# Half-width level products in a chunked delta-rule scan, with the next step's preparation in the state rounds

## The reference, cut to what matters

```python
def step(S, inp):
    r_t, w_t, k_t, v_t, a_t, b_t = inp
    Sa = jnp.einsum('bhij,bhj->bhi', S, a_t)
    S = S * w_t[:, :, None, :] + Sa[..., None] * b_t[:, :, None, :] + v_t[..., None] * k_t[:, :, None, :]
    y = jnp.einsum('bhij,bhj->bhi', S, r_t)
    return S, y
```

## Time and profile before

| what | value |
|---|---|
| median of 3 runs | 3108.72 us (3098.69 to 3109.58) |
| the profiled execution | 3100.7 us, span 3098.9 us |
| mean granted share of TensorE's 2.4 GHz | 0.947 |
| the scan's matmuls | first 741.3, last 1365.5 us |

### The profile page before, as it was taken

The page is one execution under the profiler, slowest core; times in us unless marked ns, Lnnn a source line. Parts: engine busy times, 40 slices in busy tenths (PEclk is TensorE's granted clock), DMA queues, the critical chain, the costliest instruction groups (busy, mean ns, idle before and its releaser), DMA issues. The chain is left out here.

```text
span 3098.9 us, 90983 instructions
## 1 busy us (share of the span) xinstructions
PE 2755.5 (89%) x39070; PEld 2134.9 (69%) x39070; DVE 2072.2 (67%) x3228; ACT 1459.6 (47%) x2171; POOL 324.5 (10%) x258
## 2 busy tenths in 40 slices
PE   5999987996999999974952999999999999999994
PEld 3455545665988998962532788888777777888872
DVE  3344076776656665635248888888888888888873
ACT  3211165664222232223131666666666666666663
POOL 0000000002112211204200000111101000101000
PEclk8999999998999999986975999999999999999997
DMA  4113051003221112032313999999999999999984
GB/s 127 35 41 141 20 214 43 0 0 83 68 62 44 44 50 79 4 136 85 128 69 119 333 310 315 310 316 315 307 315 303 310 301 324 317 312 306 324 273 152
DMA packets 282900, 544.78 MB, mean 176 GB/s; under 512 B 13296, under 2 KB 96880, under 8 KB 282576
## 3 DMA queue, kind: packets, MB, share of 16 engines
q1 hardware_dynamic: 273728, 505.62, 47.4%
q0 software_dynamic: 8848, 34.08, 4.2%
HBM read 487.23 MB, written 52.43 MB: 174 GB/s over the span
## 5 line engine op out<-in xcount | busy, mean ns | idle before, releaser
L1630 DVE SCALAR_TENSOR_TENSOR arena<-arena 128x1024 f16<-128x1024 f32 x768 | 904.2, 1220 | 101.5 <-ACT arena L1575 101.1
L1529 PE MATMUL ps<-arena 128*128 128x160 f16 x12288 | 855.4, 233 | 7.8 <-DVE arena L1639 3.3
L1529 PEld LDWEIGHTS ps<-arena 128*128 128x128 f16 x12288 | 851.9, 98 | 12.4 <-issue 9.6
L1575 ACT ACTIVATE arena<-arena 128x1024 f16<-128x1024 f32 x768 | 766.7, 1049 | 149.0 <-PE ps L1554 147.9
L876 PE MATMUL ps<-arena 64*64 64x64 f32 (+1 forms) x14080 | 505.5, 225 | 29.6 <-DVEq L1027 20.2
L876 PEld LDWEIGHTS ps<-arena 64*64 64x64 f32 x14080 | 487.4, 137 | 33.6 <-DVEq L1027 20.4
L1546 PE MATMUL ps<-arena 128*128 128x512 f16 x1536 | 366.6, 390 | 0.0
L389 PE MATMUL ps<-arena 128*128 128x512 f16 (+1 forms) x1584 | 285.7, 344 | 0.7 <-ACT arena L235 0.7
L1546 PEld LDWEIGHTS ps<-arena 128*128 128x128 f16 x1536 | 143.1, 100 | 185.1 <-issue 40.3
L389 PEld LDWEIGHTS ps<-arena 128*128 128x128 f16 x1584 | 154.9, 98 | 131.7 <-ACT arena L235 1.2
L1596 ACT ACTIVATE arena<-ps 128x160 f32<-128x160 f32 x256 | 77.7, 304 | 257.4 <-PE ps L1529 257.2
(11 more groups left out here) (216 smaller groups left out, 2952.9 us busy)
## 6 DMA issues: line engine op xcount, KB each, us to landing
arena<-w_gate SPq DMA_DIRECT2D x128, 1024.0 KB, 5.4
arena<-w_up SPq DMA_DIRECT2D x128, 1024.0 KB, 5.5
arena<-w_down SPq DMA_DIRECT2D x128, 1024.0 KB, 6.6
arena<-feat SPq DMA_DIRECT2D x120, 256.0 KB, 4.5
feat<-arena SPq DMA_DIRECT2D x20, 640.0 KB, 3.0
arena<-w_in SPq DMA_DIRECT2D x21, 512.0 KB, 4.0
arena<-tokens SPq DMA_DIRECT2D x20, 512.0 KB, 4.1
feat<-arena POOLq DMA_DIRECT2D x1, 7680.0 KB, 22.8
```

The lines of the kernel that those rows point to most:

```text
L1529: ins = pe.matmul(ps[:, o:o + SLOTS], part(4 * c + 2 * w + k // 4, pw) [:, k % 4, f * P:(f + 1) * P], xT2[:, px, k], start=(k == 0 and i = ...
L1575: act.activation(split[k % SPLIT][:, q * PW:(q + 1) * PW], ring[k % RING][:, q * PW:(q + 1) * PW], ACT.Copy, scale=W_SCALE).then_inc(w_hi, 1)
L1630: v.scalar_tensor_tensor(split[k % SPLIT][:, WCH + q * PW:WCH + (q + 1) * PW], ring[k % RING][:, q * PW:(q + 1) * PW], W_SCALE, split[k % ...
```

## The change

Level products stream only the columns that can be nonzero. `half_of(x, l, second)` picks, in every pair of blocks of width m, the first or the second block; `packed` gives PSUM the 32 columns side by side. The stationary operand keeps its 64 columns. `prod` becomes a buffer of its own for each level, cleared once at the start, so that ScalarE writes only the half that changes; `gu` takes its place in the state rounds. VectorE adds only the half. The width-1 level is computed from PSUM for both directions ahead of the masks, and each mask is one instruction of 1024 elements. `sums` is split: `rates` stand inside levels 2 to 4, `running` in state round 0, `blocks` in state round 1; the exponentials follow the copies of state round 0. `vb`, `bt` and `kt` have one buffer each, and the loads of `vb` come last. The tokens follow the `ax` of both directions.

```diff
-                                ins = heads(at_bank(d, 0, i), alv[d][:, l, i], inv[d][:, i])
+                                ins = heads(packed(at_bank(d, 0, i, C // 2), l), alv[d][:, l - 1, i],
+                                            half_of(inv[d][:, i], l, d == 1))
...
                             for i in range(NI):
+                                x = prod(d, l)[:, i]
                                 if l < NL:
-                                    heads(at_bank(d, 1, i), invT[d][:, i], prod[d][:, i])
-                                ins = heads(at_bank(d, 2, i), prod[d][:, i], invT[d][:, i])
+                                    heads(packed(at_bank(d, 1, i, C // 2), l), invT[d][:, i], half_of(x, l, d == 1))
+                                ins = heads(packed(at_bank(d, 2, i, C // 2), l), x, half_of(invT[d][:, i], l, d == 0))
...
-                            act.copy(flat(prod[d]), bank(4 * d)).then_inc(prod_ready[d], 1)
+                            act.copy(half_of(flat(prod(d, l)), l, d == 1),
+                                     packed(bank(4 * d, W // 2), l)).then_inc(prod_ready[d], 1)
...
                             if l < NL:
-                                v.tensor_tensor(flat(inv[d]), flat(inv[d]), bank(4 * d + 1), ALU.add)
-                            v.tensor_tensor(flat(invT[d]), flat(invT[d]), bank(4 * d + 2), ALU.add)
+                                x = half_of(flat(inv[d]), l, d == 1)
+                                v.tensor_tensor(x, x, packed(bank(4 * d + 1, W // 2), l), ALU.add)
+                            x = half_of(flat(invT[d]), l, d == 0)
+                            v.tensor_tensor(x, x, packed(bank(4 * d + 2, W // 2), l), ALU.add)
...
-                            pool.wait_ge(masks_ready[d], 3 * g + 1)
+                            pool.wait_ge(masks_ready[d], 3 * g + 2)
...
+                if g:
+                    v.wait_ge(tok_psum[d], NTOK * g)
+                v.tensor_tensor(flat(bt[d]), t1, ebk, ALU.mult)
```

More of the change, by code:

```diff
@@ L778, in build @@
         o2 += 2 * W
+        prod_a = at(o2, 2 * (NL - 1), NI, C)
+        o2 += 2 * (NL - 1) * W
         assert o2 <= E_ + 2 * KD * P + 2 * (NT + 3)
         o1 = R1
-        alv = [at(o1 + d * 6 * W, len(LEVELS), NI, C) for d in range(2)]
-        o1 += 12 * W
+        alv = [at(o1 + d * NL * W, NL, NI, C) for d in range(2)]
+        o1 += 2 * NL * W
         tokb = [at(o1 + d * W, NI, C) for d in range(2)]
@@ L788, in build @@
         o1 += 2 * W
-        prod = [at(o1 + d * W, NI, C) for d in range(2)]
+        prod_b = at(o1, 2, NI, C)
         o1 += 2 * W
+        gu = [at(o1 + d * RT * C, RT, C) for d in range(2)]
+        o1 += 2 * RT * C
         assert o1 <= B_
@@ L796, in build @@
         cin_free = [sem(f"cin_free{d}") for d in range(2)]
+        vb_in = [sem(f"vb_in{d}") for d in range(2)]
         zeroed = sem("zeroed")
@@ L836, in flat, with prod, half_of, packed @@
             return x.rearrange("p a b -> p (a b)")
+        def prod(d, l):
+            return prod_a[:, 2 * (l - 1) + d] if l < NL else prod_b[:, d]
+        def half_of(x, l, second):
+            m = LEVELS[l]
+            return x.rearrange("p (a w b) -> p a w b", w=2, b=m)[:, :, int(second)]
+        def packed(x, l):
+            return x.rearrange("p (a b) -> p a b", b=LEVELS[l])
         with nc.Block() as block:
@@ L941, in step @@
                             for f in range(RT):
-                                ins = heads(at_bank(d, 0, f), invT[d][:, 2 * f + place(d, c)], prod[d][:, f])
+                                ins = heads(at_bank(d, 0, f), invT[d][:, 2 * f + place(d, c)], gu[d][:, f])
                             ins.then_inc(u_psum[d], 1)
@@ L1055, in step @@
                             if l < NL:
-                                v.tensor_tensor(flat(inv[d]), flat(inv[d]), bank(4 * d + 1), ALU.add)
-                            v.tensor_tensor(flat(invT[d]), flat(invT[d]), bank(4 * d + 2), ALU.add)
+                                x = half_of(flat(inv[d]), l, d == 1)
+                                v.tensor_tensor(x, x, packed(bank(4 * d + 1, W // 2), l), ALU.add)
+                            x = half_of(flat(invT[d]), l, d == 0)
+                            v.tensor_tensor(x, x, packed(bank(4 * d + 2, W // 2), l), ALU.add)
                             v.drain().then_inc(inv_ready[d] if l < NL else invT_final[d], 1)
-                        if more and l in (1, 2):
-                            sums(g + 1, l - 1)
-                        if more and l in (3, 4):
-                            blocks(g + 1, l - 3)
+                            if more and 2 <= l <= 4:
+                                rates(g + 1, d, l - 2)
                     for c in range(2):
+                        if more:
+                            for d in range(2):
+                                if c == 0:
+                                    running(g + 1, d)
+                                else:
+                                    blocks(g + 1, d)
                         for d in range(2):
@@ L1087, in _ @@
                 for d in range(2):
-                    sums(0, d)
+                    running(0, d)
+                for part in range(3):
+                    for d in range(2):
+                        rates(0, d, part)
+                    v.drain()
                 for d in range(2):
```

140 lines of the change are left out of this document (77 added, 63 removed).

## The result

The changed kernel takes **3055.14 us** (median of 4 runs, 3053.32 to 3057.18); the kernel before, timed beside it, 3107.01 us (3098.69 to 3109.58). The ratio is 0.9838, with an interval of 0.9817 to 0.9858: faster by 1.6%. Its profiled execution took 3056.16 us. The medians differ by 51.9 us, the two profiled executions by 44.5: the one before was some 6 us quicker than its median. What the traces explain is the 44.5.

What follows compares the result with a forecast made beforehand. The prediction took TensorE's own work to set a scan step, with 3 to 6 us idle. Its terms, -27 + 8 - 7 - 8 + 1 = -33 us from the profiled 3100.7 us, gave 3068 us, range 3035 to 3100.

Steps and rivals of the forecast that it cites:

- Narrow products: Level products moving 32 columns: the 64-column weight load sets 58.3 ns a pair, so no gain in TensorE's own time.
- first rival: Level products at 32 moved columns are cheap, 29 ns a pair, giving 2980 us; chance 0.13.
- Front: Start of a scan step: TensorE's wait ahead of the second transposition goes, 2.7 us a step, -27 us.
- Transitions: Between levels: direction 1's update and POOL end slightly late without the tokens as cover, 0.8 us a step, +8 us.
- second rival: Broken runs on ScalarE and VectorE cost full width, level transitions take +28 us, about 3093 us; chance 0.11.
- State rounds: End of a step: `running` and `blocks` fit VectorE's idle time there, costing nothing; 5 us without the cover.
- Clock: Steps below full granted clock: the dips go with the front's 2.7 us wait, -7 us (0 to -8).
- Input loads: Loads moved to a step's end and the pair products: less "issue" idle time on TensorE, -8 us (0 to -17).
- hits half as many of these stalls: Beside the moved loads, TensorE issues a pair in 109 instead of 58 ns, so it meets half the "issue" stalls.
- Start: Before the scan: direction 0's `rates` no longer fill the wait for direction 1's loads, +1 us (0 to +2).
- third rival: 32-column products count like idle time, the clock falls, 64- and 128-column work behind slows; 3200 us at half; chance 0.07.
- better bounds: The whole kernel's time with every term at its favourable end, put at 3040 us.

Runs made afterwards that it cites:

- new_front_only: The kernel before with only the new front (width-1 level and invT of both directions ahead of the masks, POOL behind them): 3083.95 us, ratio 0.9921.
- wide_cover: The changed kernel with 64 moved columns and the tokens back between the two directions' ax, one of them at level 5: 3049.52 us, ratio 0.9813.
- after_again: The changed kernel timed once more, as a control, with nothing altered: 3054.53 us, ratio 0.9825.
- narrow_streams_only: The kernel before with level products moving only the first 32 columns, the rest left out, products added times zero: 3153.81 us, ratio 1.0129.
- old_front: The changed kernel with the front's old order (direction 0 masked first, POOL starting behind that mask), 32-column streams kept: 3135.05 us, ratio 1.0076.
- thin: The changed kernel moving 8 columns in every level product, the rest left out, products added times zero: 3243.42 us, ratio 1.0440.
- widths: The changed kernel moving 64, 32, 16, 8 and 32 columns in levels 1 to 5, the rest left out: 3142.91 us in one run.
- extra_loads: The changed kernel with ten more 256 KB transfers a step during the levels, into a spare tensor nobody reads: 3076.96 us, ratio 0.9898.

## Why the prediction was right, and where not

The time came out 13 us under the forecast, inside the range, for the reasons given; -33 us were forecast from the profiled execution, and 44.5 came. Term by term:

- **Narrow products, 0: right.** 58 ns at 8 to 64 moved columns, 33.5 with half the load, and no loss with 64 columns again. The first rival (2980 us) is out. The reading of the earlier trace rows was loose: 1.85 and 1.95 us contain the last pass's own duration, and by their starts the passes lie 112 ns apart in both rows, so an eighth of the columns saved nothing, and half of the price is 56 ns, not 58.
- **Front, -27: right.** The wait is gone in every step; put back, it costs 3.0 us a step. What the prediction looked for behind it was POOL's delivery, which was in time. It did not see that POOL's later start would stretch VectorE's preparation, had that stayed in the levels: 15 us in new_front_only. The change moves both, and its trace has no such wait.
- **Transitions, +8:** +5.6 measured against wide_cover (0.56 us a step), +6.8 by the sum below. The second rival is out: broken runs cost 422 and 377 ns.
- **State rounds, 0: right.** The wait there is 0.5 us a step as before, and VectorE's idle time took `running` and `blocks`.
- **Clock, -7: about right.** Three of eight steps were below 1.00, one of nine is now, where the prediction wanted none. The stretches at the low level sum to 20.8 us in the scan before and 6.4 after; at 7.5 us for 17.6 us of them, the 14.4 us fewer make 6.
- **Input loads, -8: mis-sized**, as the least certain term. "Issue" fell by 12.8 us. The step "hits half as many of these stalls" failed: next to none was left, 0.7 us here and 2.0 in the trace of after_again.
- **Start, +1:** +2.3.

The terms but the start forecast -34 for the scan, where -43.9 was measured. Counted from the starts of all 17,920 matmuls in each of the two scans, with a pass at 29 ns (54.5 with 128 moved columns) at the full clock, the scan's change is made up of -27.5 for the idle time of the front's listed waits, -12.8 for that under "issue", -3.9 for what the listed waits cost beyond their listed idle time, -6.5 for the low clock, and +6.8 for all that is in no list, where the transitions are. So the prediction left out the 3.9 us, 0.2 us a wait, and made the loads 5 us too small. Outside the scan, the 3.0 us behind it stand in no term. The better bounds that the prediction lists give -52, so 3049 us and not 3040; the measured time lies within either.

The **third rival** did not come about, but its mechanism is shown, and the prediction priced it on the wrong work. It took the narrow products as immune and charged only the 64- and 128-column work behind them; in fact the narrow products themselves nearly double, from 58 ns to 99 (narrow_streams_only), 101 (old_front) and 106 (thin). With 32 columns, whether it decides hangs on idle time ahead of the thin streams: the narrow streams alone, with the 2.7 us wait left in, made the kernel 1.3% slower. In the change, the new front is the cover that the narrow streams need: with the old one they cost 38 us. What the halved copies and additions of ScalarE and VectorE are worth, no run shows alone.

## What to carry to other kernels

Before narrowing what a matmul moves, set a row with few moved columns beside one with many at the same load: if the starts are as far apart, only a smaller load will help, and the thinner stream makes the clock easier to lose. When work of VectorE is reordered, look for what POOL will overlap with then, not only for whether POOL delivers in time. Parts of one change need not add up: narrow streams alone were a loss, the new front alone gave half of the gain, and a version with wide streams and the tokens left in their place was at least as fast as the whole.

## What the runs showed of the hardware

- The price of a pair of passes that its weight load sets (64 columns of float32) follows the granted clock: 58 ns a pair at 2.4 GHz, 106 at 1.2 GHz, with 8 moved columns; with 64 it is 58 (widths) and 108 (the tokens of old_front, 32 pairs from 971.04 to 974.49).
- The granted clock fell without idle time: with 8-column streams TensorE issued through the levels without a gap and still had 41 of 75 us at 1.2 GHz. With 32-column streams it fell after 2.8 us idle, in seven steps of ten, and stayed low through level 1 and the tokens behind it, where 64-column streams had it back within level 1.
- Beside transfers of 256 KB that carried none of its operands, TensorE stalled for up to 1.7 us with no semaphore to wait for (extra_loads). Each of the 90 such stalls in the scans of the kept traces ends 1.25 to 1.77 us after a 16 KB transfer of the instruction queue.
